# Experts' rows in groups of 32 on four column tiles, with the weights streamed in fp32 unsplit

## Chip, cores and metric

One core of one Trainium2 chip. The metric is the device time of the whole program in microseconds, from inputs in HBM to outputs in HBM; the median of the runs of a kernel counts.

## What is computed

One decoder layer on 512 tokens of width 1024, in fp32: two gated attention branches and then a sparse expert block. Only the expert block is touched by the change:

```python
logits = (t @ w_router) + b_router                    # t: 512 x 1024, 32 experts
top_val, top_idx = lax.top_k(logits, 4)
gate = jax.nn.softmax(top_val, axis=-1)
# for each expert e, for its rows xb:
gu = xb @ w_gate_up[e] + b_gate_up[e]                 # w_gate_up[e]: 1024 x 2048, fp32
g, u = gu[:, :1024], gu[:, 1024:]
g = jnp.minimum(g, 7.0); u = jnp.clip(u, -7.0, 7.0)
a = (u + 1.0) * (g * jax.nn.sigmoid(1.702 * g))
y = a @ w_down[e] + b_down[e]                         # w_down[e]: 1024 x 1024, fp32
# x + the sum over a token's four experts of gate * y
```

The weights of an expert are 8 MB (up projection, gate and up together) and 4 MB (down projection). With 32 experts that is 384 MB, read once.

## The kernel before, in words

The program is written out by hand: each engine has its own instruction list (`block.sync`, `block.gpsimd`, `block.scalar`, `block.vector`, `block.tensor`), and semaphores order them. Up to some 430 us it computes the attention part and the router. Then comes the expert part, in *items*: an item is an expert with up to `SLOTS` = 96 of its rows, and an expert with more rows gets a further item. In this data there are 32 items. Item 0 is written out ahead of the loops; each engine then has a loop (`Fori`) over the items, and the last item has its own version in several places.

What each engine does for item i:

- **SP** (`load_gu`, `load_dn`, lines 452 to 501) loads the weights. The up projection comes in eight chunks k of 1 MB (`gu_head` for k below 6, `gu_tail` for 6 and 7), the down projection in four chunks j of 1 MB (`wdn`). Each chunk has one buffer. In the loop's iteration i SP first waits for `gu_used[k]` at i + 1 and loads chunk k of item i + 1, for all eight k, and then waits for `dn_used[j]` at i and loads chunk j of item i, for all four j. For the last item the down chunks go to `gu_head`.
- **POOL** (`gather`, L576; `add_rows`, L583 and L586) fetches the 96 rows of an item from HBM by an indirect DMA, two items ahead, and adds an item's weighted results to `acc_dram` in HBM by another.
- **ScalarE** rounds every second block of the up chunks (`gate_up_high`, L788), all down chunks (`down_high`, L764), the rows (L793) and the activations (L770) to the fp32r format: this is the "high" part. It keeps half of the up results (`keep_rows`, L799), takes the sigmoid (L756) and weighs the results (`weigh`, L806).
- **VectorE** subtracts to obtain the "low" parts (L1163, L1212, L1157, L1203), moves the transposed rows (`move_rows`, L1152), does the rest of the activation (`activate`, L1175 on), and finds the rows of item i + 2 (`pick`, L1130, and `index`, L1141 to L1145).
- **TensorE** runs `gate_up(i)`, `turn_rows(i+1)`, `turn_gate_up(i)`, `down(i)` (L1651 to L1655). The calls of `down` lag one item: `down(i)` multiplies the activations of item i - 1. In `gate_up` half of the 2048 outputs are computed with the weights standing still and the 96 rows moving, in plain fp32 (L1584: 16 recorded passes per chunk), and half with the rows standing and the weights moving, as three products high x high, high x low, low x high (L1578 to L1580). `down` is all of the second kind (L1606 to L1608). `turn_rows` (L1549) transposes the gathered rows, `turn_gate_up` (L1599) the half of the up results that came out by rows.

TensorE's order and SP's order meet in the semaphores `gu_used[k]` (raised in `gate_up`) and `dn_used[j]` (raised in `down`). `gate_up(i)` further waits for the activations of item i - 1 to have left the banks (`gu_out`), `down(i)` for `a_ready` and for the banks to be weighed.

Elsewhere in the kernel, `route` (L1489 to L1500) computes the router's logits from products whose stationary side has 32 columns, each written to its own 32 partitions of one bank:

```python
for k in range(2 * m - 2, 2 * m + 2):
    rows = slice(k % 4 * E, (k % 4 + 1) * E)
    ins = pe.matmul(ps[rows, 6, :], w_rt[:, k, :], h2T[:, k, :], start=(m == 1), stop=(m == N_OUT - 1))
```

Of the kernel before, what the change touches and what calls it, by code (L numbers as in the profile page):

```python
# [20 lines left out]
F32 = mybir.dt.float32  # L21
# [7 lines left out]
P = 128  # L29
# [9 lines left out]
SLOTS = 96  # L39
# [15 lines left out]
def hybrid_block(nc, x, positions, norm1_g, w_in, b_forget, b_gate, q_norm_swa, k_norm_swa, sinks,  # L55
# [36 lines left out]
    with ExitStack() as ctx:  # L92
# [37 lines left out]
        stage.rewind(16 * K)  # L130
        wdn_l = stage.put("wdn_l", [P, 4, 2, D], F32R)
        stage.rewind()
        gu_tail_l = stage.put("gu_tail_l", [P, 2, F2], F32R)
# [4 lines left out]
        hold.rewind()  # L138
        gu_head_l = hold.put("gu_head_l", [P, 6, F2], F32R)
# [14 lines left out]
        xreg.rewind()  # L154
        gu_hi = xreg.put("gu_hi", [P, 4, 2, F // 2], F32R)
# [17 lines left out]
        xg = r2.put("xg", [SLOTS, D])  # L173
        xT = r2.put("xT", [P, KD, SLOTS])
        act_g = r2.put("act_g", [P, KD, SLOTS])
        act_u = r2.put("act_u", [P, KD, SLOTS])
        act_s = r2.put("act_s", [P, KD, SLOTS])
        aT = r2.put("aT", [P, KD, SLOTS])
        r2.at -= KD * SLOTS * 4
        aT_l = r2.put("aT_l", [P, KD, SLOTS], F32R)  # L180
        ysb = r2.put("ysb", [SLOTS, D])
        sel = r2.put("sel", [P, NB, SLOTS], BF16)
        zero_rows = r2.put("zero_rows", [SLOTS, D])
        r2.at -= D * 4
        gu_tok = r2.put("gu_tok", [SLOTS, 2, F // 2])
# [24 lines left out]
        work.at -= T * 4  # L210
        aT_h = work.put("aT_h", [P, KD, SLOTS], F32R)
        work.rewind()
        xT_h = work.put("xT_h", [P, KD, SLOTS], F32R)
        xT_l = work.put("xT_l", [P, KD, SLOTS], F32R)
# [12 lines left out]
        spare = const.put("spare", [P, 1])  # L227
# [40 lines left out]
        row_f = r2.put("row_f", [SLOTS, 1])  # L268
# [8 lines left out]
        idx_g = r2.put("idx_g", [SLOTS, 1], I32)  # L277
        idx_s = r2.put("idx_s", [SLOTS, 1], I32)
        idx_all = r2.put("idx_all", [SLOTS, ITEMS], I32)
        gate_all = r2.put("gate_all", [SLOTS, ITEMS])  # L280
# [3 lines left out]
        r1.rewind()  # L284
        wdn_h = r1.put("wdn_h", [P, 4, 2, D], F32R)

        ps = ctx.enter_context(nc.psum_tensor("ps", [P, 8, 512], F32))
        xT_ps_v = ps[:, 6:8, :].rearrange("p b (k s) -> p (b k) s", k=4)[:, :, 0:SLOTS]
        list_v = ps[0:SLOTS, 6, SLOTS:SLOTS + 5]
        gu_v = ps[:, 0:4, :].rearrange("p b (k s) -> p (b k) s", k=4)[:, :, 0:SLOTS]  # L290
        h2_dram = nc.dram_tensor("h2_dram", (T, D), F32, kind="Internal").ap()
        acc_dram = nc.dram_tensor("acc_dram", (T + SLOTS, D), F32, kind="Internal").ap()
        BIG = 8.0 * T
# [20 lines left out]
        last_dn_in = [sem(f"last_dn_in{j}") for j in range(4)]  # L314
        last_hi_done, last_split = sem("last_hi_done"), sem("last_split")
# [34 lines left out]
        items_ready, zero_ready = sem("items_ready"), sem("zero_ready")  # L350
# [5 lines left out]
        g_biased, gu_out, g_ready, u_ready = sem("g_biased"), sem("gu_out"), sem("g_ready"), sem("u_ready")  # L356
        sig_ready, gs_ready, a_whole = sem("sig_ready"), sem("gs_ready"), sem("a_whole")
        a_hi, a_ready = sem("a_hi"), sem("a_ready")

        xT_hi, xT_split = sem("xT_hi"), sem("xT_split")  # L360
        rows_done, rows_kept, gu_turned = sem("rows_done"), sem("rows_kept"), sem("gu_turned")


        gu_hi_done, gu_split = sem("gu_hi_done"), sem("gu_split")

        dn_hi, dn_lo = sem("dn_hi"), sem("dn_lo")
        dn_used = [sem(f"dn_used{j}") for j in range(4)]
        idx_s_ready, added, turn = sem("idx_s_ready"), sem("added"), sem("turn")
        y_ready, y_free = sem("y_ready"), sem("y_free")
# [4 lines left out]

        def split_columns(chunk):

            return chunk.rearrange("p (a b n) -> p a b n", a=2, b=2)[:, :, 1, :]

        def last_high(j):

            return gu_head_l[:, 4 + j, :] if j < 2 else gu_tail_l[:, j - 2, :]

        def gu_low(k):
            return split_columns(gu_head_l[:, k, :] if k < 6 else gu_tail_l[:, k - 6, :])

# [31 lines left out]
        def _(sp):  # L417
# [61 lines left out]
            for j in (2, 3):  # L479
                sp.wait_ge(xg_in, 16)  # L480
                load_dn(0, j)
            for k in range(KD):
                sp.wait_ge(gu_used[k], 1)
                load_gu(1, k)
            sp.wait_ge(items_ready, 1)
            last = sp.value_load(items[0:1, LAST_AT:LAST_AT + 1], min_val=E - 1, max_val=E + MAX_EXTRA - 1)
            with sp.Fori(1, last) as i:
                e1 = sp.value_load(items[0:1, bass.ds(i + 1, 1)], min_val=0, max_val=E - 1)
                e = sp.value_load(items[0:1, bass.ds(i, 1)], min_val=0, max_val=E - 1)
                for k in range(KD):  # L490
# [17 lines left out]
        def _(pool):  # L508
# [41 lines left out]
            then(g.tensor_copy(tok_f[:, :], tok_i[:, :]))  # L550
            g.tensor_scalar(spare[:, :], tok_f[:, 0:1], float(T), None, ALU.add).then_inc(consts, 1)
# [19 lines left out]
            g.memset(zero_rows[:, :], 0.0).then_inc(zero_ready, 1)  # L571
            pool.wait_ge(var_ready, 2)
            g.tensor_tensor(rstd[:, 1, :], ssq[:, 1, :], minus_half[:, 0, 0:NB], ALU.pow).then_inc(rstd_ready, 1)

            def gather():
                g.indirect_dma_start(out=xg[:, :], out_offset=None, in_=h2_dram[:, :],  # L576
                                     in_offset=bass.IndirectOffsetOnAxis(ap=idx_g[:, :], axis=0)).then_inc(xg_in, 16)

            def add_rows(n, column):

                pool.wait_ge(consts, 1)
                pool.wait_ge(y_ready, n + 1)
                g.tensor_copy(idx_s[:, :], idx_all[:, column]).then_inc(idx_s_ready, 1)  # L583
                pool.wait_ge(spare_set, 16)
                pool.wait_ge(idx_s_ready, n)
                g.indirect_dma_start(out=acc_dram[:, :],  # L586
                                     out_offset=bass.IndirectOffsetOnAxis(ap=idx_s[:, :], axis=0),
                                     in_=ysb[:, :], in_offset=None, compute_op=ALU.add).then_inc(added, 16)
                pool.wait_ge(added, n * 16)
# [26 lines left out]
        def _(act):  # L616
# [134 lines left out]

            def sigmoid(i, first=False):
# [5 lines left out]
            def down_high(n, js=range(4)):  # L758


                for j in js:
                    act.wait_ge(consts, 1)
                    act.wait_ge(dn_in[j], n * 16)
                    sc.copy(wdn_h[:, j], wdn[:, j]).then_inc(dn_hi, 1)  # L764

            def act_high(i, ahead=True):

                high, whole = (aT_h, aT) if ahead else (xT_h, xT)
                act.wait_ge(a_whole, i + 1)
                sc.copy(high[:, :, :], whole[:, :, :]).then_inc(a_hi, 1)  # L770

            def last_down_high(n, js):

                for j in js:
                    act.wait_ge(last_dn_in[j], 16)
# [904 lines left out]
```

## Time and profile before

| | |
|---|---|
| median of 3 runs | 1688.7 us (1688.68 to 1688.8) |
| the profiled execution | 1689.5 us |
| its span, first to last instruction | 1687.7 us |
| its mean granted TensorE clock | 0.987 |
| HBM read, written | 447.49 MB, 19.27 MB |

In the profile PE is TensorE's products and PEld its weight loads, which run beside them; DVE is VectorE, ACT ScalarE, POOL GpSimd and SP SyncE; a "q" behind an engine's name is its sequencer, which issues DMAs. A busy share is a share of the span. An fp32 product or a wide fp32 product shows as two recorded passes. "PEclk" is the granted clock as a share of 2.4 GHz: 1.00, or 0.50 for 1.2 GHz. The DMA share is the mean share of time in which the core's 16 DMA engines have a packet under way, and GB/s is what they moved.

### The profile page before, as it was taken

To read this page: it belongs to the slowest core of one execution; us is meant where nothing else is said; L and a number is where in the kernel's file an instruction comes from. 1 tells how busy PE (TensorE), PEld (TensorE's weight loads), DVE (VectorE), ACT (ScalarE), POOL (GpSimd) and SP (SyncE) were. 2 spreads that over 40 slices of the span, in tenths; PEclk is the share of its full clock that TensorE was granted. 3 is DMA by queue.
4 is the path that set the end of the run, shared out by engine and by line. 5 is a ranking of instruction groups with operands and counts; after the bars stand their busy time and mean duration, and the time that the engine had idled before them with its cause. 6 is when DMAs were issued, how large, how long until landed. Compare 5 with 4: busy or idle time off the path is not lost.

```text
span 1687.7 us, 28308 instructions
## 1 busy us (share of the span) xinstructions
PE 1633.1 (97%) x10608; PEld 1373.7 (81%) x10608; DVE 1080.7 (64%) x1429; ACT 769.9 (46%) x857; POOL 123.0 (7%) x171
## 2 busy tenths in 40 slices
PE   6999999999799999999999999999999999999995
PEld 6998878789588888888888888888888888888883
DVE  4125567653696677677766776677766776777663
ACT  4214354323144554555444554555444545555442
POOL 1003110000000000000000000000000000000001
PEclk9999999999799999999999999999999999999998
DMA  5332300035779999999999999999999999999982
GB/s 168 95 100 75 100 26 1 26 115 225 259 269 342 352 345 361 354 356 348 363 349 353 355 345 353 371 344 358 355 355 350 348 346 373 343 350 362 358 298 78
DMA packets 111009, 465.14 MB, mean 276 GB/s; under 512 B 11648, under 2 KB 37280, under 8 KB 78144
## 3 DMA queue, kind: packets, MB, share of 16 engines
q1 hardware_dynamic: 102784, 435.97, 70.2%
q0 software_dynamic: 7392, 25.96, 7.1%
q10 hardware_dynamic: 800, 2.77, 0.5%
q8 instruction: 21, 0.34, 0.1%
q14 instruction: 12, 0.10, 0.0%
HBM read 447.49 MB, written 19.27 MB: 277 GB/s over the span
## 4 chain that ended last, share of the span: by engine, by line
PE 95%; DVE 2%; DMA 1%; ACT 1%; issue 0%; SPq 0%; POOL 0%; POOLq 0%; ACTq 0%; DVEq 0%
PE ps L1584 28%; PE ps L1578 7%; PE ps L1580 7%; PE ps L1606 7%; PE ps L1608 7%; PE ps L1579 7%; PE ps L1607 7%; PE ps L1317 3%; PE ps L1318 3%; PE ps L1319 3%; PE ps L1326 3%; PE ps L1327 3%; PE ps L1328 3%; PE ps L1413 2%; PE ps L1440 2%; PE ps L1549 1%
## 5 line engine op out<-in xcount | busy, mean ns | idle before, releaser
L1584 PEld LDWEIGHTS ps<-xT,gu_head 128*128 128x128 f32 x3168 | 386.9, 193 | 24.6 <-issue 2.3
L1584 PE MATMUL ps<-xT,gu_head 128*128 128x96 f32 x3168 | 383.7, 275 | 1.1 <-DVE xT L1152 1.1
L1212 DVE TENSOR_TENSOR wdn_l<-wdn,wdn_h 128x2048 fp32r<-128x2048 f32 x124 | 283.2, 2284 | 23.7 <-ACT wdn_h L764 23.7
L764 ACT CAST wdn_h<-wdn 128x2048 fp32r<-128x2048 f32 x124 | 236.0, 1903 | 0.2 <-issue 0.2
L1163 DVE TENSOR_TENSOR gu_head_l<-gu_head,gu_hi 128x1024 fp32r<-128x1024 f32 x186 | 219.2, 1219 | 0.0
L1578 PE MATMUL ps<-gu_hi,xT_h 128*96 128x512 f32 x496 | 208.1, 419 | 3.7 <-DVE xT_l L1157 3.7
L788 ACT CAST gu_hi<-gu_head 128x1024 fp32r<-128x1024 f32 x186 | 185.7, 1045 | 47.4 <-DVE x_tok L1220 42.1
L1606 PE MATMUL ps<-wdn_h,aT_h 128*96 128x512 f32 x496 | 197.0, 397 | 0.0
L1580 PE MATMUL ps<-gu_hi,xT_l 128*96 128x512 f32 x496 | 195.8, 395 | 0.0
L1608 PE MATMUL ps<-wdn_h,aT_l 128*96 128x512 f32 x496 | 194.8, 393 | 0.0
L1607 PE MATMUL ps<-wdn_l,aT_h 128*96 128x512 f32 x496 | 194.2, 391 | 0.0
L1152 DVE TENSOR_TENSOR xT<-ps,vcol 128x768 f32<-128x768 f32 x32 | 30.7, 958 | 228.6 <-PE ps L1549 228.6
L799 ACT COPY gu_tok<-ps 96x512 f32<-96x512 f32 x62 | 33.0, 582 | 300.4 <-PE ps L1580 300.4
L1579 PE MATMUL ps<-gu_head_l,xT_h 128*96 128x512 f32 x372 | 146.1, 393 | 0.0
L864 DVE TENSOR_TENSOR st_l<-st_w,st_h 128x2048 fp32r<-128x2048 f32 x25 | 57.3, 2292 | 121.5 <-ACT st_h L634 121.5
L1584 PEld LDWEIGHTS ps<-xT,gu_tail 128*128 128x128 f32 x1056 | 127.5, 192 | 7.0
L1584 PE MATMUL ps<-xT,gu_tail 128*128 128x96 f32 x1056 | 126.3, 273 | 0.0
L770 ACT CAST aT_h<-aT 128x768 fp32r<-128x768 f32 x31 | 25.8, 832 | 193.9 <-DVE aT L1200 193.9
L1580 PEld LDWEIGHTS ps<-gu_hi,xT_l 128*96 128x96 f32 x496 | 80.2, 162 | 34.9
L1608 PEld LDWEIGHTS ps<-wdn_h,aT_l 128*96 128x96 f32 x496 | 79.9, 161 | 34.9
L1607 PEld LDWEIGHTS ps<-wdn_l,aT_h 128*96 128x96 f32 x496 | 80.2, 162 | 32.4
L1606 PEld LDWEIGHTS ps<-wdn_h,aT_h 128*96 128x96 f32 x496 | 80.0, 161 | 32.0
(312 smaller groups left out, 2601.3 us busy)
## 6 DMA issues: line engine op xcount, KB each, us to landing
gu_head<-in_w_gate_up_dram SPq DMA_DIRECT2D x192, 1024.0 KB, 7.2
wdn<-in_w_down_dram SPq DMA_DIRECT2D x124, 1024.0 KB, 8.0
gu_tail<-in_w_gate_up_dram SPq DMA_DIRECT2D x64, 1024.0 KB, 8.3
st_w<-in_w_in_dram SPq DMA_DIRECT2D x17, 1024.0 KB, 5.4
st_w<-in_w_out_dram SPq DMA_DIRECT2D x4, 1024.0 KB, 5.1
gu_head<-in_w_down_dram SPq DMA_DIRECT2D x4, 1024.0 KB, 7.2
x_tok<-in_x_dram SPq DMA_DIRECT2D x4, 512.0 KB, 5.5
st_w<-in_w_o_swa_dram SPq DMA_DIRECT2D x4, 512.0 KB, 3.5
```

The costliest lines, as they stand in the source:

```text
L764: sc.copy(wdn_h[:, j], wdn[:, j]).then_inc(dn_hi, 1)
L788: sc.copy(gu_hi[:, k % 4], split_columns(gu_chunk(k))).then_inc(gu_hi_done, 1)
L864: v.tensor_tensor(st_l[:, g % 2], st_w[:, g % 2], st_h[:, g % 2].bitcast(F32), ALU.subtract).then_inc(split_lo, 1)
L1163: v.tensor_tensor(gu_low(k), split_columns(gu_chunk(k)), gu_hi[:, k % 4].bitcast(F32), ALU.subtract).then_inc(gu_split, 1)
L1212: v.tensor_tensor(wdn_l[:, j], wdn[:, j], wdn_h[:, j].bitcast(F32), ALU.subtract).then_inc(dn_lo, 1)
L1578: pe.matmul(dst, xT_h[:, k, :], w_h, start=(k == 0), stop=False)
L1579: pe.matmul(dst, xT_h[:, k, :], w_l, start=False, stop=False)
L1580: ins = pe.matmul(dst, xT_l[:, k, :], w_h, start=False, stop=(k == KD - 1))
L1584: ins = pe.matmul(gu_v[:, f], gu_chunk(k)[:, f * P:(f + 1) * P], xT[:, k, :], start=(k == 0 and f % 4 == 0), stop=(k == KD - 1), skip_grou ...
L1606: pe.matmul(dst, a_h[:, f, :], w_h, start=(f == 0), stop=False)
L1607: pe.matmul(dst, a_h[:, f, :], w_l, start=False, stop=False)
L1608: return pe.matmul(dst, a_l[:, f, :], w_h, start=False, stop=(f == KD - 1))
```

## The change

- The rows of an item stay 96, in three groups of 32. In `gate_up` the rows stand (32 columns) and the weights move, in plain fp32; the four quarters of 512 outputs go to the four column tiles, each to its 32 partitions of bank n for group n. `down` does the same with halves of 512 outputs: two groups by two halves in bank 4, and in bank 5 the third group by two halves by even and odd k, which are added when the results are weighed.
- All splits into high and low parts go from the expert part, with their buffers and semaphores.
- `turn_gate_up` transposes all three banks (12 transposes of 128 x 128), after ScalarE has copied them (`keep_rows`).
- The rows are gathered and added as halves of 512 elements: 128 and 64 half rows, so two indirect DMAs for each gather and each add. `pick`, `index`, `lists` give an index for each half row; `weigh` and the new `weigh_odd` give `y_a` and `y_b`.
- SP's loop loads the four down chunks of item i first and then the eight up chunks of item i + 1. The last item has no version of its own any more.

The core of the diff, cut:

```diff
-SLOTS = 96
+GROUP = 32
+N_GROUPS = 3
+SLOTS = GROUP * N_GROUPS
...
+            def gu_free(k, n):
+
+                if k < KD - 1:
+                    sp.wait_ge(gu_used[k], n)
+                else:
+                    sp.wait_ge(bank_done, n * N_GROUPS)
+
+            for k in range(KD):
+                gu_free(k, 1)
+                load_gu(1, k)
             with sp.Fori(1, last) as i:
                 e1 = sp.value_load(items[0:1, bass.ds(i + 1, 1)], min_val=0, max_val=E - 1)
                 e = sp.value_load(items[0:1, bass.ds(i, 1)], min_val=0, max_val=E - 1)
-                for k in range(KD):
-                    sp.wait_ge(gu_used[k], i + 1)
-                    load_gu(e1, k)
                 for j in range(4):
                     sp.wait_ge(dn_used[j], i)
                     load_dn(e, j)
-
+                for k in range(KD):
+                    gu_free(k, i + 1)
+                    load_gu(e1, k)
             e = sp.value_load(items[0:1, bass.ds(last, 1)], min_val=0, max_val=E - 1)
             for j in range(4):
-                sp.wait_ge(gu_used[j], last + 1)
-                sp.dma_start(gu_head[:, j, :].rearrange("p (k n) -> p k n", k=2),
-                             w_dn_v[bass.ds(e, 1), j].rearrange("a p k n -> (a p) k n")).then_inc(last_dn_in[j], 16)
+                sp.wait_ge(dn_used[j], last)
+                load_dn(e, j)
...
             def gather():
-                g.indirect_dma_start(out=xg[:, :], out_offset=None, in_=h2_dram[:, :],
-                                     in_offset=bass.IndirectOffsetOnAxis(ap=idx_g[:, :], axis=0)).then_inc(xg_in, 16)
+                g.indirect_dma_start(out=xg_a[:, :], out_offset=None, in_=h2_rows[:, :],
+                                     in_offset=bass.IndirectOffsetOnAxis(ap=idx_g[:, 0:1], axis=0)).then_inc(xg_in, 16)
+                g.indirect_dma_start(out=xg_b[:, :], out_offset=None, in_=h2_rows[:, :],
+                                     in_offset=bass.IndirectOffsetOnAxis(ap=idx_g[0:HD, 1:2], axis=0)).then_inc(xg_in, 16)
...
+            def keep_rows(i, first=False):
+
+                if not first:
+                    act.wait_ge(gu_turned, i * N_GROUPS)
+                for n in range(N_GROUPS):
+                    act.wait_ge(bank_done, i * N_GROUPS + (n + 1))
+                    sc.copy(gu_tok[:, n, :], ps[:, n, :]).then_inc(rows_kept, 1)
...
+            with act.Fori(1, n_items) as i:
                 keep_rows(i)
                 sigmoid(i)
                 weigh(i, bass.ds(i - 1, 1))
...
+                for n in range(N_GROUPS):
+                    s = slice(n * GROUP, (n + 1) * GROUP)
+                    halves = ps[:, n, :].rearrange("p (a k s) -> p a k s", a=2, s=GROUP)
+                    dve.wait_ge(gu_turned, i * N_GROUPS + (n + 1))
+                    v.tensor_tensor(act_g[:, :, s], halves[:, 0], bc(at[:, 0:KD], 2, GROUP), ALU.add)
+                    ins = v.tensor_tensor(act_u[:, :, s], halves[:, 1], bc(at[:, KD:2 * KD], 2, GROUP), ALU.add)
+                ins.then_inc(gu_out, 1)
...
+            with dve.Fori(1, n_items) as i:
                 e = dve.value_load(items[0:1, bass.ds(i, 1)], min_val=0, max_val=E - 1)
                 pick(i + 2)
+                index(i + 2)
+                move_rows(i + 1)
+                activate(i, e)
+                weigh_odd(i, bass.ds(i - 1, 1))
+            weigh_odd(n_items, bass.ds(n_items - 1, 1))
...
             def gate_up(i, first=False):
 
+                pe.wait_ge(xT_ready, i + 1)
+                if not first:
                     pe.wait_ge(gu_out, i)
                 for k in range(KD):
+                    pe.wait_ge(gu_in[k], i * 16 + 16)
+                    for n in range(N_GROUPS):
+                        for j in range(4):
+                            ins = pe.matmul(ps[j * GROUP:(j + 1) * GROUP, n, :], xT[:, k, n * GROUP:(n + 1) * GROUP],
+                                            gu_chunk(k)[:, j * 512:(j + 1) * 512], start=(k == 0), stop=(k == KD - 1))
                         if k == KD - 1:
+                            ins.then_inc(bank_done, 1)
+                    if k < KD - 1:
+                        ins.then_inc(gu_used[k], 1)
...
+            def down(n):
 
                 pe.wait_ge(a_ready, n)
+                pe.wait_ge(yb_ready, n)
+                pe.wait_ge(ya_ready, n)
                 for j in range(4):
+                    pe.wait_ge(dn_in[j], n * 16)
                     for k in (0, 1):
+                        for u in range(4):
+                            ins = pe.matmul(ps[u * GROUP:(u + 1) * GROUP, 4, :],
+                                            aT[:, 2 * j + k, u // 2 * GROUP:(u // 2 + 1) * GROUP],
+                                            wdn[:, j, k, u % 2 * 512:(u % 2 + 1) * 512],
+                                            start=(j == 0 and k == 0), stop=(j == 3 and k == 1))
+                    for u in range(4):
+                        ins = pe.matmul(ps[u * GROUP:(u + 1) * GROUP, 5, :], aT[:, 2 * j + u // 2, 2 * GROUP:],
+                                        wdn[:, j, u // 2, u % 2 * 512:(u % 2 + 1) * 512], start=(j == 0), stop=(j == 3))
                     ins.then_inc(dn_used[j], 1)
...
+            def turns(i):
+
+                lists(i + 2)
+                turn_rows(i + 1)
+                turn_gate_up(i)
...
             with pe.Fori(1, n_items) as i:
                 gate_up(i)
-                turn_rows(i + 1)
-                turn_gate_up(i)
+                turns(i)
                 down(i)
-            last_down(n_items)
+            down(n_items)
```

## Rows read from the trace of the kernel before

**Rows 1.** The page: busy time and share of each engine, and 40 slices.

```profile
PE 1633.1 (97%) x10608; PEld 1373.7 (81%) x10608; DVE 1080.7 (64%) x1429; ACT 769.9 (46%) x857; POOL 123.0 (7%) x171
...
PE   6999999999799999999999999999999999999995
...
PEclk9999999999799999999999999999999999999998
DMA  5332300035779999999999999999999999999982
```

**Rows 2.** Windows: one expert, from one load of the last up chunk to the next.

```profile
core 0: us, PE busy (x) PEld busy (x) DVE busy (x) ACT busy (x) POOL busy (x), PEclk, DMA share, GB/s
1003.65:1041.43 37.78, 37.78 (x246) 31.31 (x245) 26.48 (x29) 19.28 (x18) 2.56 (x3) 1.00 0.99 349
```

**Rows 3.** Waits of SP's queue: who waited for whom, total us, times, longest.

```profile
SPq L454 <- PE ps L1584: 639.2, 248, 8.6
SPq L458 <- PE ps L1608: 309.6, 120, 3.6
```

**Rows 4.** Timeline of TensorE, then windows, at the loop's start.

```profile
479.84 0.83 PE L1549 MATMUL ps<-ident,xg 96*128 96x96 f32 x8
484.40 0.74 PE L1578 MATMUL ps<-gu_hi,xT_h 128*96 128x512 f32 x1 [3.73 <-DVE xT_l L1157]
484.94 0.63 PE L1579 MATMUL ps<-gu_head_l,xT_h 128*96 128x512 f32 x1
...
489.74 0.45 PE L1578 MATMUL ps<-gu_hi,xT_h 128*96 128x512 f32 x1
...
484.40:489.10 4.70, 4.70 (x16) 3.86 (x17) 3.77 (x6) 1.68 (x2) 0.00 (x0) 0.50 0.30 85
489.10:495.00 5.90, 5.90 (x45) 5.11 (x45) 4.90 (x8) 5.71 (x5) 0.00 (x0) 1.00 0.64 193
```

**Rows 5.** Timeline of TensorE at the router: whole burst, first four passes.

```profile
417.03 1.07 PE L1498 MATMUL ps<-h2T,w_rt 128*32 128x512 f32 x8
...
417.03 0.64 PE L1498 MATMUL ps<-h2T,w_rt 128*32 128x512 f32 x4
```

**Rows 6.** L1559, four passes in one tile: timeline, and durations (min/median/max ns).

```profile
455.70 1.98 PE L1559 MATMUL ps<-b_dn,gateT 32*128 32x512 f32 x4
...
L1559 PE MATMUL ps<-b_dn,gateT x12: 587/587/692, 455.7 to 468.5; 32*128 32x512 f32 x12
```

**Rows 7.** Timeline of TensorE: transposes of 128 and of 96 rows.

```profile
416.06 1.04 PE L1486 MATMUL ps<-ident,x_tok 128*128 128x128 f32 x8
...
1003.32 0.83 PE L1549 MATMUL ps<-ident,xg 96*128 96x96 f32 x8
```

**Rows 8.** ScalarE's copies, L799: durations (min/median/max ns).

```profile
L799 ACT COPY gu_tok<-ps x62: 581/582/584, 510.5 to 1644.7; 96x512 f32<-96x512 f32 x62
```

**Rows 9.** The page's costliest groups: busy us, mean ns, idle before.

```profile
L1212 DVE TENSOR_TENSOR wdn_l<-wdn,wdn_h 128x2048 fp32r<-128x2048 f32 x124 | 283.2, 2284 | 23.7 <-ACT wdn_h L764 23.7
L764 ACT CAST wdn_h<-wdn 128x2048 fp32r<-128x2048 f32 x124 | 236.0, 1903 | 0.2 <-issue 0.2
L1163 DVE TENSOR_TENSOR gu_head_l<-gu_head,gu_hi 128x1024 fp32r<-128x1024 f32 x186 | 219.2, 1219 | 0.0
L788 ACT CAST gu_hi<-gu_head 128x1024 fp32r<-128x1024 f32 x186 | 185.7, 1045 | 47.4 <-DVE x_tok L1220 42.1
```

**Rows 10.** POOL's gather issues, L576 (ns), and the timeline of the end.

```profile
L576 POOL DMA_INDIRECT xg<-h_dram,idx_g x34: 912/927/1191, 434.3 to 1647.4; - x34
...
1671.19 1.11 ACT L806 ACTIVATE ysb<-ps,gate_all 96x1024 f32<-96x1024 f32 x1 [11.59 <-PE ps L1629]
...
1673.44 1.45 POOL L586 DMA_INDIRECT acc_dram<-ysb,idx_s  x1 [0.79 <-POOL idx_s L583]
```

**Rows 11.** Landing of chunks (L458, L454 twice), and window of a full queue.

```profile
L458 SPq DMA_DIRECT2D wdn<-in_w_down_dram x4: 372/375/383, 516.5 to 524.8; - x4
...
DMA to landing us min/median/max: 5.5/5.5/5.5
...
DMA to landing us min/median/max: 4.7/4.8/4.9
...
DMA to landing us min/median/max: 7.0/7.4/8.4
...
380.00:392.00 12.00, 12.00 (x103) 12.00 (x102) 3.99 (x3) 3.50 (x9) 0.00 (x0) 1.00 1.01 419
```

More of the change, by code:

```diff
@@ L549, in _ @@
             g.tensor_copy(iota_f[:, :], iota_i[:, :])
[L550 to L551 removed]
+            g.tensor_copy(tok_f[:, :], tok_i[:, :]).then_inc(consts, 1)
             pool.wait_ge(var_ready, 1)
@@ L844, in _ @@
-            with act.Fori(1, last) as i:
-                act_item(i)
-            act_item(last, ahead=False)
-            n_items = act.value_load(items[0:1, N_AT:N_AT + 1], min_val=E, max_val=E + MAX_EXTRA)
             weigh(n_items, bass.ds(n_items - 1, 1))
@@ L1166, in last_low @@
[L1166 to L1173 removed]
+                v.tensor_tensor(xT[:, :, 0:2 * GROUP], xT_a, bc(vcol[:, 8:8 + KD], 2, 2 * GROUP), ALU.mult)
+                v.tensor_tensor(xT[:, :, 2 * GROUP:], xT_b, bc(vcol[:, 8:8 + KD], 2, GROUP), ALU.mult).then_inc(xT_ready, 1)
@@ L1195, in activate, with weigh_odd @@
                 dve.wait_ge(u_ready, i + 1)
-                if not first and ahead:
+                if not first:
                     dve.wait_ge(dn_used[3], i)
-                whole, high, low = (aT, aT_h, aT_l) if ahead else (xT, xT_h, xT_l)
-                v.scalar_tensor_tensor(out=whole[:, :, :], in0=act_u[:, :, :], scalar=1.0, in1=act_g[:, :, :],
-                                       op0=ALU.add, op1=ALU.mult).then_inc(a_whole, 1)
-                dve.wait_ge(a_hi, i + 1)
-                v.tensor_tensor(low[:, :, :], whole[:, :, :], high[:, :, :].bitcast(F32),
-                                ALU.subtract).then_inc(a_ready, 1)
-                if not ahead:
-                    last_low(range(4))
-            def down_low(n, js=range(4)):
-                for j in js:
-                    dve.wait_ge(dn_hi, n * 4 + (j + 1))
-                    v.tensor_tensor(wdn_l[:, j], wdn[:, j], wdn_h[:, j].bitcast(F32),
-                                    ALU.subtract).then_inc(dn_lo, 1)
+                v.scalar_tensor_tensor(out=aT[:, :, :], in0=act_u[:, :, :], scalar=1.0, in1=act_g[:, :, :],
+                                       op0=ALU.add, op1=ALU.mult).then_inc(a_ready, 1)
+            def weigh_odd(n, column):
+                dve.wait_ge(y_odd_ready, n)
+                v.scalar_tensor_tensor(out=y_b[:, :], in0=ps[0:HD, 5, :],
+                                       scalar=gate_all[0:HD, column, 1:2].rearrange("p a n -> p (a n)"),
+                                       in1=y_odd[:, :], op0=ALU.mult, op1=ALU.add).then_inc(yb_ready, 1)
             def add_bias(c):
@@ new lines, in gate_up @@
+                    if first and k in (2, 4, 6):
+                        bias_rows(k // 2)
+            def turn_gate_up(i):
+                for n in range(N_GROUPS):
+                    pe.wait_ge(rows_kept, i * N_GROUPS + (n + 1))
+                    out_v = ps[:, n, :].rearrange("p (j c s) -> p c j s", j=4, c=4)
+                    for c in range(4):
+                        ins = pe.transpose(out_v[:, c], gu_tok[:, n, c * P:(c + 1) * P], ident[:, :])
+                    ins.then_inc(gu_turned, 1)
```

357 lines of the change are left out of this document (109 added, 248 removed).

## The prediction

> **What bounds the kernel now.** I read the page's busy shares and the slices first [rows 1]: TensorE is busy 97% of the span, its clock is full, and from slice 12 the DMA engines are nearly always occupied as well. The windows of one expert come next [rows 2]: an expert takes 37.78 us, in which TensorE is busy all the time, VectorE 26.5 and ScalarE 19.3 us, and the DMA engines show a share of 0.99 at 349 GB/s. The waits of SP's queue [rows 3] say which of the two sets the pace: 248 weight loads waited for TensorE to finish with the old chunk, 639 us in all, and 120 more 310 us, while nothing on TensorE waits for weights. So TensorE bounds the loop, and the loads follow it chunk by chunk. Of the 12 chunks of 1 MB for an expert, eight belong to the up projection and four to the down projection. The loop starts at 484.4 us [rows 4] and stands for 31 of the 32 experts.
>
> **TensorE's work after.** Per expert there are 96 fp32 products for the up projection (8 k, 3 groups, 4 column tiles) and 48 for the down projection, each of 512 columns and each recorded as two passes. The kernel has the same form once already, the router's four products on four column tiles: eight passes with 32 weight columns took 1.07 us, and the first four of them together 0.64 us [rows 5]. One tile's passes in a row take 0.43 us each: four took 1.98, the first of them 0.69, so (1.98-0.69)/3 [rows 6]. Eight passes in a row would be 3.4 us, so in the router the four tiles did run at once, each with other moving data. A quartet is then 2 x 0.43 = 0.86 us in a long stream. From the other side, if every quartet drains before the next begins, it costs the router's whole 1.07. I take 0.86, because the passes of one tile already follow each other without a drain [rows 6], and keep 1.07 for the range. Up projection: 24 quartets, 20.7 us (25.7). Down: 12 quartets, 10.4 us (12.8).
>
> What an expert needs beside: eight transposes of rows, twelve of the up projection, and eight list products. A 128-wide transpose costs 1.04/8 = 0.13 us with its end, eight narrower ones took 0.83 [rows 7]. That is 0.9 + 1.6, overlapping a little, plus some 0.5 for lists: 3.0 us. The copies of three banks by ScalarE are 0.58 us each [rows 8]; two lie under the last chunk, the third under lists and row transposes. Bounds: 2.4 and 4. Sum without any wait: 20.7+3.0+10.4 = 34.1 us, 3.7 less than 37.78.
>
> **What goes from the other engines.** Splits of weights, rows and activations leave VectorE and ScalarE: the eight wdn and gate_up groups alone are 283+219 us of VectorE and 236+186 of ScalarE [rows 9]. They lie beside TensorE's work, so they bring nothing by themselves. What replaces them (six bias adds of 256 elements, 256-wide selection, the halved weighing) is under 10 us per expert on either engine, under the 20 us of up products. The activation of one expert still has all of the next up projection before its down projection needs it; only after the last expert does its final operation, 0.96 us, wait for the down products before it, 1.5 us with the hand-over. Gather and add become two indirect DMAs each. POOL pays 0.93 us per gather and 1.45 per add issue [rows 10], hidden in the loop; at the very end one more issue, 1.5 us, is exposed.
>
> **The order of the loads.** This is the part that decides. SP's queue is in order. Before, an expert's turn loads the next expert's eight up chunks, each as soon as TensorE is done with it, and then four down chunks. After, the four down loads stand first, and each waits for dn_used of down(i). TensorE runs gate_up(i), turns, down(i), gate_up(i+1). The up chunks of expert i+1 are free from gate_up(i) on, but SP reaches their loads only when down(i) has used its last chunk, just as TensorE wants the first of them. Nothing else is left for TensorE there. Queued behind SP's wait are all eight up loads; waiting for them is the whole of TensorE.
>
> The wait: the last down chunk and the first up chunk must both land. Down chunks issued 2.77 us apart in the first expert, near the 2.6 of the new pace, landed after 5.5 us; up chunks in a quiet queue after 4.8, in a full one after 7.0 to 8.4 [rows 11]. The first up chunk lands one chunk later. With a full queue the engines moved 419 GB/s [rows 11], so 1.05 MB take 2.5 us. The add of the previous expert (0.39 MB written) falls between: 0.7 us as its share. Wait: 5.5+2.5+0.7 = 8.7 us; bounds 4.8+2.5 = 7.3 and some 10. The other seven land 2.5 us apart, the last some 18 us after the first, ahead of TensorE, which needs 2.6 per chunk.
>
> The Trainium skill (DMA: Bandwidth & Descriptors, "Where 436 GB/s comes from") puts the limit of loads from HBM at about 358 GB/s per core. By it a chunk would take 2.9 us, the wait would grow by 0.4, the chunks would come slower than TensorE takes them, and the time would be some 30 us more. The trace's 419 GB/s over 12 us speaks against it.
>
> **The clock.** Before the first item of the loop TensorE stood idle for 3.73 us; the products after it took twice as long, and windows show a granted clock of 0.50 (1.2 GHz) until 489.1, 4.7 us after work began, and 1.00 (2.4 GHz) from there [rows 4]. An 8.7 us hole per expert repeats this. 4.7 us at half speed give back 2.35 us of work, so the up projection takes 23.05 us. Zero stays the other end.
>
> **Sum.** Period: 10.4 + 8.7 + 23.05 + 3.0 = 45.15 us, 7.4 more than before. The lead-in: the first up projection runs as 24 quartets instead of 128 products of 96 columns, but is paced by VectorE's bias adds; I take the start of gate_up(1) at 478 instead of 484.4 (no row shows it; bounds 472 and 486). gate_up(1) finds its weights loaded. Then 20.7 + 3.0 to the start of down(1), 30 periods of 45.15 = 1354.5, down(31) 10.4, down(32) 10.4+1.5. The end from the last weighing at 1671.2 on is 16.5 us [rows 10] and becomes 18. Together 478+23.7+1354.5+10.4+11.9+18 = 1896.5 us of span. The profiled run took 1689.5 us with a span of 1687.7, and lies 0.8 above the median of 1688.7; so plus 1.0: 1898 us. Low end: wait 7.3, no clock loss, turns 2.4, so a period of 40.8, and the loop's start at 472: 1760. High end: quartets of 1.07 and a period of 52.5: 2128.
>
> **Rivals.** (a) *The loads come in time, faster.* Place: the hole between down(i) and gate_up(i+1). Without it the period is 34.1: 478+23.7+1023+40.3 = 1565 us. It turns at a period of 38.2, that is a hole of 4.1 us with full clock. For it speaks that DMA has 34.1 us for 12 chunks of 2.5 and the small transfers; against it that the code lets no up load start earlier, and 4.8 us is the least landing seen. 6%, most of it near 1580 to 1680.
> (b) *Tiles overlap less.* Quartets of 1.07 give a period of 12.8+8.7+28.05+3.0 = 52.5 and 2128 us. What the trace has is one burst of eight passes [rows 5]; a stream may queue. 10%. The Trainium skill (TensorE: Matmul & The Clock Gate, "Measured speedup vs the span model") gives 2.38 for three column tiles instead of 3; at that efficiency a quartet is 1.08 us, this rival's price.
> (c) *The tiles take turns.* The change then doesn't do what it says: 144 products x 0.86 = 124 us per expert, some 4500 us. The router's burst speaks against it [rows 5]. 3%.
> (d) *Loads delay the up projection throughout.* If chunks come every 2.9 to 3.1 us beside other traffic, the period is 46 to 49: 1925 to 2015 us. 12%, inside the range.
>
> **How the numbers follow.** The forecast as worked out has 67%, with the clock loss between none and full; (a) 6%, (b) 10%, (c) 3%, (d) 12%, no visible change 2%. The range 1760 to 2128 leaves out (a), (c) and part of (b). This kernel can be told from no change at 0.2%. Faster 0.06, same 0.02, slower 0.92.
>
> **What would show it.** The waits after: TensorE at the first gate_up product waits for the DMA of gu_head some 30 times, 8 to 9 us each; SP waits for down's last chunk with no wait at the gate_up loads behind it; windows of an expert near 45 us, with TensorE busy about 36 and DMA share near 0.8; a granted clock of 0.5 for 4 to 6 us after each hole; quartets starting 0.86 us apart. Wrong it is if gate_up starts right behind down, or if a quartet takes 1 us or more.

## The result and the profile after

The changed kernel takes 1882.35 us (median of 4 runs, 1879.65 to 1887.68) against 1688.75 for the kernel before in the same comparison: a ratio of 1.1148, 95% interval 1.112 to 1.1176. Forecast were 1898 us and a range of 1760 to 2128. The profiled execution took 1884.43 us with a span of 1882.3, 2.1 above the median; its mean granted clock is 0.906 where it was 0.987.

The page, lines that answer to [rows 1], then the chain that ended last, by engine, and two issue lines (issues, KB each, us to landing):

```profile
PE 1583.6 (84%) x12848; PEld 727.9 (39%) x12848; DVE 514.1 (27%) x1196; ACT 288.0 (15%) x484; POOL 207.6 (11%) x239
...
PE   6999999997877778888888888888777887888885
...
PEclk9999999997998888888888888888888888888888
DMA  5223200258388777887777777777777777787775
...
PE 82%; DMA 12%; DVE 2%; issue 1%; SPq 1%; ACT 1%; POOL 0%; DVEq 0%; POOLq 0%; ACTq 0%
...
gu_head<-in_w_gate_up_dram SPq DMA_DIRECT2D x192, 1024.0 KB, 13.5
wdn<-in_w_down_dram SPq DMA_DIRECT2D x128, 1024.0 KB, 4.9
```

TensorE fell from 97% to 84% of the span, and the DMA engines, nearly full before, now stand at 7 or 8 tenths. Neither is full, although 447 MB still have to come in: each waits for the other. VectorE and ScalarE lost more than half of their work, 1080.7 to 514.1 and 769.9 to 288.0 us, and nothing of that shows in the time.

The waits name who waits for whom, first TensorE's, then those of SP's queue (total us, times, longest), where [rows 3] had 639.2 us at the up loads and 309.6 at the down loads:

```profile
PE ps L1480 <- DMA gu_head<-in_w_gate_up_dram: 240.3, 30, 10.7
...
SPq L430 <- PE ps L1512: 1132.2, 124, 32.6
...
SPq L426 <- PE ps L1480: 21.6, 7, 4.3
```

SP now waits at the down loads alone, up to 32.6 us each; behind that wait the up loads follow almost without one. One expert shows why it hurts, in the timelines of TensorE and of SP:

```profile
1006.14 1.04 PE L1512 MATMUL ps<-wdn,aT 128*32 128x512 f32 x8
1014.87 18.46 PE L1480 MATMUL ps<-gu_head,xT 128*32 128x512 f32 x144 [7.68 <-DMA gu_head<-in_w_gate_up_dram]
1033.15 5.32 PE L1480 MATMUL ps<-gu_tail,xT 128*32 128x512 f32 x48
1038.41 0.35 PE L1446 MATMUL ps<-row_tab,sel 128*128 x8
...
1041.04 1.50 PE L1507 MATMUL ps<-wdn,aT 128*32 128x512 f32 x12
...
1007.38 0.37 SPq L430 DMA_DIRECT2D wdn<-in_w_down_dram  x1
1007.94 2.94 SPq L426 DMA_DIRECT2D gu_head<-in_w_gate_up_dram  x6
1011.06 0.92 SPq L426 DMA_DIRECT2D gu_tail<-in_w_gate_up_dram  x2
```

TensorE's last down product ends at 1007.18. Only then does SP issue the last down load and, 0.56 us later, the first of eight up loads in a row, for buffers the last of which TensorE had left 13 us before, at the end of the up projection (the turns and the down projection lie between). TensorE stands idle for 7.68 us. The windows of the same expert, cut at the hole, the up projection, the turns and the down projection (columns as in [rows 2]), and a second cut of the up projection where the clock rises:

```profile
1007.46:1014.86 7.40, 0.00 (x0) 0.00 (x0) 2.70 (x6) 1.32 (x2) 3.24 (x3) 0.69 1.03 421
1014.86:1038.40 23.54, 23.53 (x192) 6.16 (x192) 0.00 (x0) 1.17 (x2) 0.00 (x0) 0.88 0.81 315
1038.40:1041.04 2.64, 2.64 (x33) 2.23 (x29) 1.90 (x8) 0.59 (x1) 0.55 (x1) 1.00 0.00 0
1041.04:1051.82 10.78, 10.51 (x97) 3.01 (x96) 3.74 (x9) 0.89 (x2) 1.41 (x2) 1.00 0.76 264
...
1014.86:1020.00 5.14, 5.13 (x26) 1.18 (x30) 0.00 (x0) 0.00 (x0) 0.00 (x0) 0.50 1.05 345
```

The four windows make 44.36 us where [rows 2] had 37.78. The DMA engines are full in the hole (421 GB/s), and stand still later, in the turns, while TensorE is busy. In the first 5.14 us after the hole the granted clock is 0.50, that is 1.2 GHz, as after the wait in [rows 4].

### The profile page after: what moved, and what is told of

It reads as the page before. It is cut to its first block, busy times and chain, and to the rows that moved or that the text cites. A ratio compares the mean times of both kernels' runs of the same rounds, so it can differ in the third digit from the quotient of the medians.

```text
span 1882.3 us, 31477 instructions
## 1 busy us (share of the span) xinstructions
PE 1583.6 (84%) x12848; PEld 727.9 (39%) x12848; DVE 514.1 (27%) x1196; ACT 288.0 (15%) x484; POOL 207.6 (11%) x239
## 4 chain that ended last, share of the span: by engine, by line
PE 82%; DMA 12%; DVE 2%; issue 1%; SPq 1%; ACT 1%; POOL 0%; DVEq 0%; POOLq 0%; ACTq 0%
PE ps L1480 40%; PE ps L1507 12%; DMA gu_head<-in_w_gate_up_dram 11%; PE ps L1512 6%; PE ps L1222 3%; PE ps L1223 3%; PE ps L1224 3%; PE ps L1495 2%; PE ps L1231 2%; PE ps L1233 2%; PE ps L1232 2%; PE ps L1318 2%; PE ps L1345 1%; PE ps L1456 1%; PE ps L1334 1%
## 5 line engine op out<-in xcount | busy, mean ns | idle before, releaser
L1480 PE MATMUL ps<-gu_head,xT 128*32 128x512 f32 x4608 | 582.6, 670 | 245.4 <-DMA gu_head<-in_w_gate_up_dram 240.3
L1480 PEld LDWEIGHTS ps<-gu_head,xT 128*32 128x32 f32 x4608 | 150.7, 122 | 675.6 <-issue 388.6
L1507 PE MATMUL ps<-wdn,aT 128*32 128x512 f32 x2048 | 244.9, 595 | 2.1 <-DVE y_b L1129 2.1
L744 ACT COPY gu_tok<-ps 128x512 f32<-128x512 f32 x96 | 56.2, 585 | 921.6 <-PE ps L1480 921.6
L1480 PE MATMUL ps<-gu_tail,xT 128*32 128x512 f32 x1536 | 170.6, 592 | 0.0
L1512 PE MATMUL ps<-wdn,aT 128*32 128x512 f32 x1024 | 134.2, 596 | 0.0
L1507 PEld LDWEIGHTS ps<-wdn,aT 128*32 128x32 f32 x2048 | 63.5, 110 | 142.9 <-issue 142.9
L1222 PE MATMUL ps<-st_h,hT_h 128*128 128x256 f32 x288 | 82.4, 286 | 2.0 <-DVE hT_l L808 2.0
L1223 PE MATMUL ps<-st_l,hT_h 128*128 128x256 f32 x288 | 82.2, 285 | 0.0
L1224 PE MATMUL ps<-st_h,hT_l 128*128 128x256 f32 x288 | 82.2, 285 | 0.0
L1512 PEld LDWEIGHTS ps<-wdn,aT 128*32 128x32 f32 x1024 | 33.5, 110 | 77.1 <-issue 77.1
L1222 PEld LDWEIGHTS ps<-st_h,hT_h 128*128 128x128 f32 x288 | 56.0, 194 | 2.4 <-DVE hT_l L808 2.3
```

What stands on the lines that cost most here:

```text
L744: sc.copy(gu_tok[:, n, :], ps[:, n, :]).then_inc(rows_kept, 1)
L1222: pe.matmul(dst, xh[:, k], wh[:, k], start=(k == 0), stop=False)
L1223: pe.matmul(dst, xh[:, k], wl[:, k], start=False, stop=False)
L1224: ins = pe.matmul(dst, xl[:, k], wh[:, k], start=False, stop=(k == n - 1))
L1480: ins = pe.matmul(ps[j * GROUP:(j + 1) * GROUP, n, :], xT[:, k, n * GROUP:(n + 1) * GROUP], gu_chunk(k)[:, j * 512:(j + 1) * 512], start=( ...
L1507: ins = pe.matmul(ps[u * GROUP:(u + 1) * GROUP, 4, :], aT[:, 2 * j + k, u // 2 * GROUP:(u // 2 + 1) * GROUP], wdn[:, j, k, u % 2 * 512:(u ...
```

## The experiments

The theory: the order of the loads costs the time, by a hole (forecast 8.7 us, 7.7 in the expert shown) and a low clock after it; the products themselves became faster. The rivals: the tiles overlap less than assumed, or loads are slow throughout. A diff is against the changed kernel unless it says otherwise; line numbers shift by a few where lines were added. The kernel with the up chunks first ran four times, the others once each, in two later sessions, in which the kernel before took 1692.38 us (median of 7) and 1690.07 (one run) instead of 1688.75. So a difference of a few us between two times says little; periods are read from the traces.

### Up chunks first

```diff
             with sp.Fori(1, last) as i:
...
-                for j in range(4):
-                    sp.wait_ge(dn_used[j], i)
-                    load_dn(e, j)
                 for k in range(KD):
                     gu_free(k, i + 1)
                     load_gu(e1, k)
+                for j in range(4):
+                    sp.wait_ge(dn_used[j], i)
+                    load_dn(e, j)
```

> The kernel after, with SP's loop turned back to the old order: eight up chunks of item i+1 first, then four down chunks of item i. Theory (the order of the loads costs the whole loss): no hole between down(i) and gate_up(i+1), the clock stays at 1.00, the period is TensorE's 34.1 us; 478+23.7+30x34.1+40.3 = about 1565 us, up to 1600 if the loads press now and then. Rival (the DMA engines were full before as well, share 0.99 at 349 GB/s, and set the pace as soon as TensorE is faster): the period stays at 37.5 us or so, about 1670 us. Rival (the tiled form itself is the slower one): over 1750 us.

Measured: 1560.66 us (4 runs, 1559.02 to 1561.19) against 1692.38 for the kernel before beside it: 0.9217, interval 0.9193 to 0.924. The window of one expert, then the seam between down and up in TensorE's timeline:

```profile
1001.90:1035.60 33.70, 33.70 (x320) 11.49 (x316) 8.34 (x21) 3.98 (x6) 5.21 (x5) 1.00 1.02 397
...
1020.62 1.04 PE L1512 MATMUL ps<-wdn,aT 128*32 128x512 f32 x8
1021.48 14.78 PE L1480 MATMUL ps<-gu_head,xT 128*32 128x512 f32 x136
```

One expert takes 33.70 us, all of it TensorE's, at full clock, and the up products follow 0.86 us after the start of the last eight passes, without a wait. So the hole and the low clock both came from the order: 321.7 us between these two kernels (325 if each is measured against the kernel before beside it). It is the fastest kernel of the study and has everything of the change but the new order. The rivals about tiles and slow loads are out: quartets run 0.86 us apart, and 397 GB/s suffice. That share of 1.02 also says what comes next: the DMA engines are as full as TensorE.

### The kernel before with the down chunks first

```diff
 (against the kernel before)
-                for k in range(KD):
-                    sp.wait_ge(gu_used[k], i + 1)
-                    load_gu(e1, k)
                 for j in range(4):
...
+                for k in range(KD):
+                    sp.wait_ge(gu_used[k], i + 1)
+                    load_gu(e1, k)
```

> The kernel before, with only SP's loop in the new order (four down chunks first, then eight up chunks). Theory: the same hole opens, and longer by the two splits of the first chunk: 5.5+2.5+0.7+1.05+1.2 = 11 us, and 2 us by the clock, so a period of about 51 us for 30 items: 1689 + 30 x 13 = about 2080 us. Rival (the split engines' queues absorb it, since they already stand between landing and product): less than 5 us per item, under 1840 us.

Measured: 2248.14 us, 556 to 559 above the kernel before; the expected value was too low by 168 us. Window of an expert and TensorE's two waits, then TensorE's timeline at the second of them and VectorE's up to it:

```profile
1000.00:1056.40 56.40, 43.18 (x244) 35.46 (x244) 26.38 (x30) 19.39 (x19) 2.56 (x3) 0.83 0.62 236
...
PE ps L1578 <- DVE gu_head_l L1163: 298.9, 30, 10.2
PE ps L1540 <- DVE sel L1130: 109.4, 31, 4.1
...
1054.73 0.61 PE L1540 MATMUL ps<-row_tab,sel 128*96 x4 [3.27 <-DVE sel L1130]
...
1048.51 1.23 DVE L1163 TENSOR_TENSOR gu_head_l<-gu_head,gu_hi 128x1024 fp32r<-128x1024 f32 x1 [1.26 <-ACT gu_hi L788]
1050.64 0.96 DVE L1200 SCALAR_TENSOR_TENSOR aT<-act_u,act_g 128x768 f32<-128x768 f32 x1
1052.49 0.96 DVE L1203 TENSOR_TENSOR aT_l<-aT,aT_h 128x768 fp32r<-128x768 f32 x1 [0.90 <-ACT aT_h L770]
1053.69 0.81 DVE L1130 TENSOR_SCALAR sel<-iota_f,slot_tab 128x96 bf16<-128x96 f32 x4 [0.24 <-issue]
```

The hole is there, 10 us at 30 experts, but there is a second wait. In TensorE's program the list products for item i + 2 (L1540) stand behind chunk 1 of the up projection and wait for VectorE's selection (`pick`, L1130). In VectorE's program the selection stands behind the low parts of chunks 0 to 3 and the end of the activation. VectorE could begin the low part of chunk 3 only at 1048.51, when that chunk had landed and ScalarE had cast it, and so came to the selection at 1053.69. TensorE was through with chunk 1 at 1051.47 and stood for 3.27 us, although the low part of chunk 2 had been ready since 1047.25; its passes afterwards took 0.63 us again instead of 0.39. An expert takes 18.6 us longer than in [rows 2]: 10.0 for the hole, 3.3 for the second wait, and 5.4 because TensorE's own work takes 43.18 us instead of 37.78 at a mean clock of 0.83. Expected were 11 for the hole and 2 for the clock. What the expected value left out is that other engines' work stands in order behind the late chunks as well, and brings TensorE a second wait and a second fall of the clock.

With the two results the four combinations stand side by side (us):

| | up chunks first | down chunks first |
|---|---|---|
| products and splits of before | 1688.75 | 2248.14 |
| products of the change | 1560.66 | 1882.35 |

### Keeping TensorE's clock up through the hole

```diff
                     pe.wait_ge(gu_out, i)
+                    for m in range(8):
+                        for j in range(4):
+                            pe.matmul(ps[j * GROUP:(j + 1) * GROUP, 3, 16:T], ident[:, j * GROUP:(j + 1) * GROUP],
+                                      upto[:, 16:T], start=True, stop=True)
                 for k in range(KD):
```

> The kernel after, with eight quartets of products without use (496 columns of a constant, 0.83 us each) ahead of each gate_up's wait for its weights, so that TensorE works in the hole; the output is not touched. Theory (the clock's fall costs 2.35 us per item, beside the hole of 7 to 8 us itself): the granted clock stays at 1.00 in the loop, the up projection takes 20.7 instead of 23.5 us, the hole stays; 30 x 2.5 = 75 us less, about 1807 us. Rival (the up projection is paced by the landing of its chunks, so that the clock costs nothing): within 15 us of 1882.

Measured: 1871.43 us, 10.9 less than the changed kernel and 64 more than expected. The mean clock is 0.985, so the dummy products did their work, but most of the time didn't come back. The number is the one that the rival named (within 15 us of 1882). TensorE's timeline, then windows over the hole, over the first two chunks and over the next four:

```profile
1004.56 6.84 PE L1478 MATMUL ps<-upto,ident 128*32 128x496 f32 x64
1012.43 2.78 PE L1484 MATMUL ps<-gu_head,xT 128*32 128x512 f32 x24 [1.03 <-DMA gu_head<-in_w_gate_up_dram]
1015.95 2.78 PE L1484 MATMUL ps<-gu_head,xT 128*32 128x512 f32 x24 [0.74 <-DMA gu_head<-in_w_gate_up_dram]
1019.42 10.51 PE L1484 MATMUL ps<-gu_head,xT 128*32 128x512 f32 x96 [0.68 <-DMA gu_head<-in_w_gate_up_dram]
...
1004.56:1012.43 7.87, 6.84 (x68) 1.95 (x60) 2.80 (x6) 1.37 (x2) 3.24 (x3) 1.00 1.02 418
1012.43:1019.42 6.99, 5.56 (x48) 1.36 (x49) 0.00 (x0) 0.00 (x0) 0.00 (x0) 1.00 1.04 356
1019.42:1029.74 10.32, 10.32 (x96) 3.13 (x100) 0.00 (x0) 0.00 (x0) 0.00 (x0) 1.00 1.02 429
```

Once TensorE is at full clock, the landing of the chunks is the next limit: chunks 1 and 2 land 3.5 us apart, where 2.6 are needed, and in this stretch the engines move 356 GB/s at a full share, against 418 and 429 around it. The stretch is the one in which the two indirect adds are under way: in the changed kernel POOL issues them 3 and 5 us into the hole, and they land 9.8 us later (median). That they are the cause is tried next.

### Without the adds, cold and warm

Two kernels: both leave out the two indirect adds, the second has the dummy products as well.

```diff
                 pool.wait_ge(idx_s_ready, n)
-                g.indirect_dma_start(out=acc_rows[:, :], ...
-                g.indirect_dma_start(out=acc_rows[:, :], ...
-                pool.wait_ge(added, n * 32)
                 pool.sem_inc(y_free, 1)
```

> The kernel after without the two indirect DMAs that add an item's results to HBM (so the experts' part is missing from the output). In the kept-warm run the first three up chunks landed 3.5 us apart and the others 2.5, and both adds were under way just then. Theory (the adds widen these two gaps, and the cold TensorE, 5.1 us for the first chunk, doesn't notice): the gaps become 2.5 us, the up projection stays at 23.5 us, the hole shrinks by at most 0.7 us; with some 7 us less at the very end 1855 to 1880 us. Rival (the adds are a main part of the hole): the hole falls to 5 us or less, under 1810 us.

> As the run before (no adds, the experts' part missing from the output), and TensorE kept at work in the hole by the eight quartets without use. Theory (the clock's fall costs 2.35 to 2.9 us per item, and the adds' slower landings hid that in the kept-warm run): the up projection takes 20.7 us, 30 x 2.8 = 80 us less than the run without adds. Rival (the clock is no cost here at all, whatever the landings): within 20 us of the run without adds.

Measured: 1875.80 us cold (the clock falls in the hole), inside the expected 1855 to 1880, and 1807.23 warm (it is kept up), 69 us less where 80 were expected; the up projection takes 20.7 us, as expected. TensorE's timeline of the one, then of the other, with a window over its first chunks:

```profile
1013.18 18.34 PE L1473 MATMUL ps<-gu_head,xT 128*32 128x512 f32 x144 [7.74 <-DMA gu_head<-in_w_gate_up_dram]
1031.34 5.32 PE L1473 MATMUL ps<-gu_tail,xT 128*32 128x512 f32 x48
```

```profile
1022.64 6.84 PE L1471 MATMUL ps<-upto,ident 128*32 128x496 f32 x64
1030.82 15.66 PE L1477 MATMUL ps<-gu_head,xT 128*32 128x512 f32 x144 [1.34 <-DMA gu_head<-in_w_gate_up_dram]
1046.29 5.33 PE L1477 MATMUL ps<-gu_tail,xT 128*32 128x512 f32 x48
...
1030.82:1038.00 7.18, 7.18 (x68) 2.21 (x72) 0.00 (x0) 0.00 (x0) 0.00 (x0) 1.00 1.01 423
```

Without the adds the up products follow one another without a wait from the first chunk on, and the engines move 423 GB/s where they moved 356.

| | adds made | adds left out |
|---|---|---|
| clock falls in the hole | 1882.35 (44.45) | 1875.80 (44.37) |
| kept up | 1871.43 (43.87) | 1807.23 (41.88) |

In brackets stands the period, from the start of down(1) to that of down(31) over 30, each from one trace; the trace of the changed kernel is of its execution of 1884.43 us. Leaving out the adds alone is worth 0.08 us per expert, keeping up the clock alone 0.58, both together 2.57. The four runs of the changed kernel lie 8 us apart, 0.27 per expert, so 0.08 can't be told from nothing. (Leaving out the adds takes 7 us from the kernel whose clock falls; most of that is the last pair, at the very end; and the dummy products delay the start of down(1) by 6 us.) The two losses lie on the same microseconds: while TensorE runs at 1.2 GHz it takes 5.1 us per chunk, so chunks 3.5 us apart are early enough; once it is fast, it waits for them instead. The hole itself is 7.74 us without the adds and 7.68 with them; over 30 experts the waits make 234.0 and 240.3 us, so the adds' share in it is 0.2 us at most.

### Two and four up chunks early

```diff
+                for k in range(2):
+                    gu_free(k, i + 1)
+                    load_gu(e1, k)
                 for j in range(4):
                     sp.wait_ge(dn_used[j], i)
                     load_dn(e, j)
-                for k in range(KD):
+                for k in range(2, KD):
```

The second kernel has 4 in the place of both 2.

> The kernel after with SP's loop in the order: up chunks 0 and 1 of item i+1, the four down chunks of item i, up chunks 2 to 7 of item i+1. Theory (the hole is a lag of 8.0 us, of which each chunk that is there already covers TensorE's 2.58 us): the wait moves to chunk 2 and is 8.0-5.2 = 2.8 us, and some 1 us more at the next two, while the adds land; the clock stays up; a period of 37.5 to 38.5, about 1690 us. Rival (any up chunk behind the down loads costs the whole lag): over 1800 us.

> As the run before, but with up chunks 0 to 3 ahead of the down chunks and 4 to 7 behind. Theory: four chunks cover 10.3 us, more than the 8.0 of the lag, so no wait is left; 1561 to 1575 us, as with all eight ahead. Rival (with half the loads issued late the DMA engines idle in between and can't catch up, since eight ahead already moved 397 GB/s at a share of 0.99): over 1620 us.

Measured: 1710.79 and 1575.08 us. TensorE's timeline with two early, for one expert and for the start of another, with a window over the latter:

```profile
1022.04 5.33 PE L1483 MATMUL ps<-gu_head,xT 128*32 128x512 f32 x48
1029.92 2.78 PE L1483 MATMUL ps<-gu_head,xT 128*32 128x512 f32 x24 [2.54 <-DMA gu_head<-in_w_gate_up_dram]
1033.32 2.78 PE L1483 MATMUL ps<-gu_head,xT 128*32 128x512 f32 x24 [0.62 <-DMA gu_head<-in_w_gate_up_dram]
1036.78 5.36 PE L1483 MATMUL ps<-gu_head,xT 128*32 128x512 f32 x48 [0.67 <-DMA gu_head<-in_w_gate_up_dram]
...
1106.31 12.31 PE L1483 MATMUL ps<-gu_head,xT 128*32 128x512 f32 x96 [2.48 <-DMA gu_head<-in_w_gate_up_dram]
...
1106.31:1111.31 5.00, 5.00 (x32) 1.42 (x36) 0.00 (x0) 0.00 (x0) 0.00 (x0) 0.66 1.06 351
```

Two chunks bridge 5.2 us of a wait of 7.7; 2.54 are left in the first expert, and the slow landings beside the adds cost 1.3 more. But only 8 of the 30 experts run like it. In the other 22 the clock fell after the wait at chunk 2, as in the second expert shown (0.66 over 5 us), and the chunks behind it were then in time or nearly so, as in the changed kernel. So the expected 1690 us was missed by 21, and the expectation that the clock stays up failed: its mean is 0.961. The waits for weights make 99.2 us, 3.3 per expert, and the period is 38.68 where it is 33.67 with all up chunks first. Four chunks bridge the whole wait: 11.7 us of waits for weights in the run, a period of 34.17, and a time at the upper end of the expected 1561 to 1575. So the time follows the number of up chunks that stand ahead of SP's wait for down (44.45, 38.68, 34.17 and 33.67 us for 0, 2, 4 and 8), and not something else in the loop's form.

### Four products in one tile

Against the kernel with the up chunks first:

```diff
                     for u in range(4):
-                        ins = pe.matmul(ps[u * GROUP:(u + 1) * GROUP, 5, :], aT[:, 2 * j + u // 2, 2 * GROUP:],
+                        ins = pe.matmul(ps[0:GROUP, 5, :], aT[:, 2 * j + u // 2, 2 * GROUP:],
```

> As the first of these, but the four products of the third row group in down are all written to column tile 0 instead of four tiles (so bank 5 holds a wrong sum, and that part of the output is not the reference's). Theory (the four tiles run at once; one alone takes 0.43 us per pass): four sets of eight passes take 3.43 instead of 0.86 us, 10.3 us more per item, 32 x 10.3 = 330 us more than the first of these. Rival (products on different tiles share the array and gain less, about half): under 170 us more.

Measured: 1888.23 us, 327.6 above the kernel it was made from. The line's passes and the idle time of the weight load before them (us, times), first spread over four tiles, then in one:

```profile
L1512 PE MATMUL ps<-wdn,aT x1024: 592/592/1061, 507.8 to 1540.4; 128*32 128x512 f32 x171
...
  issue: 76.9, 256
```

```profile
L1512 PE MATMUL ps<-wdn,aT x1024: 592/592/592, 507.8 to 1867.5; 128*32 128x512 f32 x171
...
  issue: 326.2, 1024
```

A pass takes 592 ns in both; what changes is when the next may start. In one tile the weight load waits before each of the 1024 passes, on four tiles before every fourth. Passes in one tile start 0.43 us apart, as in [rows 6], eight of them 3.43 us. For the 128 quartets of this line that is (3.43 - 0.86) x 128 = 329 us, as measured. So four column tiles are worth a factor of four in these 128 quartets, and the 0.86 us holds over the whole stream of 9216 passes. Rival (b) falls. The Trainium skill (TensorE: Matmul & The Clock Gate, "Measured speedup vs the span model") has 2.38 for three column tiles. By an estimate from that figure a quartet would take 1.08 us; this trace, with four tiles in a long stream, has 0.86 and doesn't agree.

## Why the prediction came out right, point by point

- **What bounds, and the place of the loss.** As forecast: 30 waits of TensorE at the first up product, SP waiting at the down loads alone, a hole at every expert and a granted clock of 0.50 for 5.1 us after it. Undoing the order alone takes all of it back.
- **Quartets of 0.86 us**: 0.86, shown by the timeline and by the one-tile kernel. Up projection at full clock: 33.70 - 2.63 - 10.33 = 20.74 (20.7), with the turns and the down projection as they stand in the kernel with the up chunks first. Down: 10.33 (10.4).
- **The turns**: 2.64 us, forecast 3.0 with bounds of 2.4 and 4. The lists took 0.21 us instead of 0.5, the row transposes 0.96 (0.9), the twelve transposes 1.46 (1.6).
- **The hole**: 7.6 to 8.4 us in 27 of the 30 experts and 9.5 to 10.7 in three, 8.0 in the mean; forecast 8.7. Why three are longer stays open. The term was mis-sized in two places. The last down chunk lands after 4.9 us, not 5.5, and the adds take nothing from the first up chunk: they are issued only 2.3 us and more after it. What is left is 0.2 us to the issue, 4.9, and 2.5 for the chunk behind it, 7.6. (The forecast calls 4.8 us the least landing seen; its own rows have 4.7.)
- **Other up chunks 2.5 us apart**: wrong for chunks 1 and 2, which come 3.5 apart beside the adds, right for the rest. In the changed kernel nobody notices, since TensorE is at half clock then. The term of 0.7 us for the adds was put in the wrong place.
- **The clock's 2.35 us**: the up projection took 23.54, that is 2.8 more than at full clock. But the step took it for a loss that stands by itself. Kept warm, TensorE won 0.58 us per expert (44.45 to 43.87); only with the adds gone as well is the loss there in full, 2.49 us (44.37 to 41.88).
- **The period**: from down(1), which starts at 506.33, to down(31) at 1839.76 are 30 periods of 44.45 us, forecast 45.15. That is 21.1 us less than in the sum. Part of this closeness is luck: the hole (-0.7 us per expert) and the turns (-0.4) were put too high, the clock (+0.5) too low, and the errors partly cancel.
- **Lead-in and end**: gate_up(1) starts at 481.34, forecast 478. It has to wait 4.00 us for VectorE's bias adds, and so begins at half clock, 22.4 us for 20.7. down(1) thus came 4.6 us later than in the sum. The last down projection waited 2.06 us, forecast 1.5, for `y_b` and not for the activation, and its first passes ran at half clock again; the end from down(31) on took 42.5 us, forecast 40.3. With the periods: 4.6 - 21.1 + 2.2 = -14.3, and 1896.5 - 14.3 = 1882.2.
- **Rival (a)**, loads in time at 1565 us, was the right price for a kernel with the order of before: 1560.66. **Rival (d)** holds for two chunks only. The Trainium skill (DMA: Bandwidth & Descriptors, "Where 436 GB/s comes from") puts loads at some 358 GB/s; the runs show 421 in the hole and 397 over a whole expert, so they don't agree; only one core runs here, and no run shows two. Nor do the 30 us that the forecast gave for it follow from its own terms: 0.4 us at the wait and 0.05 at the up projection make some 14, an estimate from the page's figure. No such delay came. The 356 GB/s beside the adds are near its figure, but they are a stretch of mixed reads and writes.

What stays open: whether the adds slow the loads by their writes, by reading back what they add to, or by their small packets. That wasn't tried. Nor was it tried why the clock fell in some experts with two early chunks and not in others.

## What to carry to other kernels

When one queue loads for two consumers that run in turn, put next in the queue what becomes free first and is wanted first; a wait for the later consumer holds up everything behind it, however free those buffers are. Here that was worth 321.7 us against a gain of 128 us from everything else in the change. Look at what stands in order behind the late transfer on every other engine before carrying such a hole over to another kernel, and where two losses lie on the same microseconds, try them removed alone and together before adding them up.

## What the runs showed of the chip that was not expected

- Four column tiles with different moving data overlap fully in a long stream: 0.86 us for eight passes of 512 columns, 3.43 in one tile (shown for the third row group of the down projection).
- Beside two indirect adds of 0.39 MB in all, the DMA engines show a full share but move 356 GB/s instead of 418 to 429, and a 1 MB chunk takes 3.5 us instead of 2.5.
- The clock fell after the wait of 2.06 us before the last down projection. With two chunks early it fell after the wait at chunk 2 in 22 experts and stayed up in 8, and waits of nearly the same length did either: 2.48 us above, with 0.66 after it, and 2.54 us, with 1.00. The windows after the wait of 2.06 us, in the changed kernel, and after that of 2.54:

```profile
1852.33:1857.00 4.67, 4.67 (x28) 1.32 (x32) 0.00 (x0) 0.00 (x0) 2.04 (x3) 0.63 0.56 218
```

```profile
1029.92:1036.78 6.86, 5.56 (x49) 1.35 (x49) 0.00 (x0) 0.00 (x0) 0.00 (x0) 1.00 1.04 356
```

The rows don't say what makes the difference; all three waits follow at least 10 us of products in a row.
